# The last head pair's scan is moved into the output stage's program, with part of the output stage's first heads spread over its chunks

## The reference, cut to what matters

```python
def step(state, inp):                      # over the chunks of a sequence, per head
    qd, qkc, uc, wc, kd, gl = inp
    v_new = uc - einsum('bhcd,bhde->bhce', wc, state)
    o = einsum('bhcd,bhde->bhce', qd, state) + einsum('bhcs,bhse->bhce', qkc, v_new)
    state = state * gl[..., None, None] + einsum('bhcd,bhce->bhde', kd, v_new)
    return state, o
...
o = rms_norm(o, norm_w) * silu(z)          # per head, over its 128 channels
return o.reshape(bsz, t, nh * dh) @ w_out  # then x = x + gate * y, rms_norm, the second block
```

## Time and profile before

| what | value |
|---|---|
| time, median of three runs | 2098.21 us (2095.83 to 2099.14) |
| time of the profiled execution | 2094.25 us |
| its span, first to last instruction | 2092.4 us |
| PE busy | 1981.1 us, 95% of the span |
| DVE busy | 1291.3 us, 62% |
| ACT busy | 865.7 us, 41% |
| mean granted TensorE clock | 0.983 |

### The profile page before, as it was taken

One profiled execution on the slowest core, in us unless ns is written; L12 is line 12 of the kernel. 1 busy time (PEld: TensorE's weight loads), 2 busy tenths in 40 slices (PEclk: granted clock), 3 DMA queues, 4 the chain that ended last, 5 costly groups with the idle time before them and its releaser, 6 DMA issues.

```text
span 2092.4 us, 29549 instructions
## 1 busy us (share of the span) xinstructions
PE 1981.1 (95%) x11256; PEld 1629.1 (78%) x11256; DVE 1291.3 (62%) x2447; ACT 865.7 (41%) x1392; POOL 136.8 (7%) x114
## 2 busy tenths in 40 slices
PE   5889999999999999969999899999999999999998
PEld 3667878888887878857776788787787888888877
DVE  7776778796869686749625755445455436633543
ACT  5644353544354443149402333535443438600321
POOL 0020202021111212000000000000000000000000
PEclk8999999999999999989999999999999999999999
DMA  7222323232323242548213131211313115211232
GB/s 286 83 76 70 96 80 107 66 101 71 105 68 102 71 121 67 170 146 289 89 43 139 44 103 32 89 72 61 101 32 111 70 73 210 90 51 42 88 112 81
DMA packets 130252, 204.47 MB, mean 98 GB/s; under 512 B 56853, under 2 KB 88341, under 8 KB 129089
## 3 DMA queue, kind: packets, MB, share of 16 engines
q1 hardware_dynamic: 130112, 202.58, 30.6%
HBM read 156.22 MB, written 42.11 MB: 95 GB/s over the span
## 4 chain that ended last, share of the span: by engine, by line
PE 43%; DVE 6%; ACT 3%; issue 2%; DMA 1%; SPq 0%; DVEq 0%; ACTq 0%
PE m_job L1708 5%; PE m_job L1710 5%; PE m_job L1709 5%; PE e_b L2421 4%; PE e_b L2422 4%; PE e_b L2423 4%; PE p_out L1352 2%; PE p_out L1353 2%; PE p_out L1354 2%; PE p_s L1991 1%; PE e_b L2492 1%; PE e_b L2491 1%; PE e_b L2490 1%; PE p_t L1980 1%; PE p_sc L1968 1%
## 5 line engine op out<-in xcount | busy, mean ns | idle before, releaser
L795 PE MATMUL p_job<-h_hi,w_hi 128*128 128x512 f32 x768 | 321.9, 419 | 16.7 <-DVE h_lo L185 15.2
L797 PE MATMUL p_job<-h_hi,w_lo 128*128 128x512 f32 x768 | 302.9, 394 | 0.0
L796 PE MATMUL p_job<-h_lo,w_hi 128*128 128x512 f32 x768 | 302.5, 394 | 0.0
L1708 PE MATMUL m_job<-h_hi,m_hi 128*128 128x512 f32 x576 | 244.4, 424 | 5.0 <-issue 4.2
L1710 PE MATMUL m_job<-h_hi,m_lo 128*128 128x512 f32 x576 | 227.3, 395 | 0.0
L1709 PE MATMUL m_job<-h_lo,m_hi 128*128 128x512 f32 x576 | 226.1, 392 | 0.0
L795 PEld LDWEIGHTS p_job<-h_hi,w_hi 128*128 128x128 f32 x768 | 146.1, 190 | 58.3 <-issue 16.2
L796 PEld LDWEIGHTS p_job<-h_lo,w_hi 128*128 128x128 f32 x768 | 146.2, 190 | 35.1 <-issue 7.6
L797 PEld LDWEIGHTS p_job<-h_hi,w_lo 128*128 128x128 f32 x768 | 146.0, 190 | 31.3
L633 ACT ACTIVATE pre<-p_job 128x512 f32<-128x512 f32 x96 | 56.8, 592 | 177.5 <-PE p_job L797 174.3
L1708 PEld LDWEIGHTS m_job<-h_hi,m_hi 128*128 128x128 f32 x576 | 109.1, 189 | 25.1 <-issue 5.4
(11 more groups left out here) (399 smaller groups left out, 4224.4 us busy)
## 6 DMA issues: line engine op xcount, KB each, us to landing
w_raw<-in_w SPq DMA_DIRECT2D x49, 512.0 KB
m_raw<-in_w SPq DMA_DIRECT2D x49, 512.0 KB, 3.6
rows<-grows SPq DMA_DIRECT2D x32, 512.0 KB, 6.7
ada<-in_ada_w SPq DMA_DIRECT2D x8, 1024.0 KB, 5.6
z_scr<-pre SPq DMA_DIRECT2D x16, 512.0 KB, 2.6
o_scr<-oT SPq DMA_DIRECT2D x64, 128.0 KB, 1.8
ob<-o_scr SPq DMA_DIRECT2D x16, 512.0 KB, 4.7
zb<-z_scr SPq DMA_DIRECT2D x16, 512.0 KB, 4.9
```

What stands on the lines that cost most here:

```text
L795: nc.tensor.matmul(bank, hi, h_hi[:, k, cut], start=(k == 0), stop=False)
L796: nc.tensor.matmul(bank, hi, h_lo[:, k, cut], start=False, stop=False)
L797: last = nc.tensor.matmul(bank, lo, h_hi[:, k, cut], start=False, stop=(k == KD - 1))
L1708: nc.tensor.matmul(bank, hi, h_hi[:, k, cut], start=(k == 0), stop=False)
```

## The change

The last pair's scan leaves `plan(8)` (the steps stand there only while a next pair exists) and becomes a function `stage_last_scan`, called inside the output stage's streams. Its order on each engine is that of a chunk before; after chunk c, at a named place, a hook of the output stage runs. The first program no longer waits for the stored z and o at its end; SP waits for them where they are needed. Heads 0 to 2 get buffers of their own for squares, heads 0 and 1 for inverse norms and sums (`p_out[4:6]`), and the first two weight splits go to `m_hi`, `m_lo`.

```diff
+def stage_last_scan(nc, io, keep, t):
...
+            for a in range(2):                                   # ACT, chunk c
...
+                nc.scalar.activation(vn[:, a, :], p_head[a][:, P:2 * P], ACT.Copy).then_inc(vn_done, 1)
+            hook(c, 0)
...
+            nc.scalar.activation(oT[:, c % 2], p_query, ACT.Copy).then_inc(o_done, 1)
+            hook(c, 1)
...
+            last.then_inc(write_ready, 1)                        # PE, end of chunk c
+            hook(c)
...
+            for a in range(2):                                   # DVE, chunk c
...
+                                               vb[:, c, a, :], ALU.mult, ALU.add).then_inc(d_done, 1)
+            hook(c)
...
+                nc.vector.scalar_tensor_tensor(S[:, a, :], S[:, a, :], gl[:, c, a:a + 1], p_head[a][:, 2 * P:3 * P],
+                                               ALU.mult, ALU.add).then_inc(s_done, 1)
```

```diff
+            def ahead(c, place):          # ACT; squares are Square and a rounding Copy
+                if (c, place) == (1, 0):   square(0)
+                elif (c, place) == (1, 1): high_square(0)
+                elif (c, place) == (2, 0): square(1)
+                elif (c, place) == (2, 1): high_square(1)
+                elif (c, place) == (3, 0): logarithm(0)
+                elif (c, place) == (3, 1): exponent(0)
+                elif (c, place) == (4, 0): root()
+                elif (c, place) == (5, 0): logarithm(1)
+                elif (c, place) == (5, 1): exponent(1)
+                elif (c, place) == (6, 0): high(0)
+                elif (c, place) == (6, 1): square(2)
+                elif (c, place) == (7, 0): high_square(2)
...
+            def ahead(c):                 # PE
+                if c == 2:
+                    pe.wait_ge(fn_set, 2)
+                    sums(0)
+                elif c == 4:
+                    sums(1)
...
+            def ahead(c):                 # DVE
+                if c == 1:   constants()
+                elif c == 2: low_square(0)
+                elif c == 3: gated(0)
+                elif c == 4: low_square(1)
+                elif c == 5: scaled(0)
+                elif c == 6: gated(1)
+                elif c == 7: low_part(0)
```

```diff
+            scan["scalar"](act, ahead)
+            high(1)
+            for n in range(2, V_HEADS):
+                logarithm(n)
+                exponent(n)
+                if n + 1 < V_HEADS:
+                    square(n + 1)
+                    high_square(n + 1)
+                high(n)
...
+            scan["vector"](dve, ahead)
+            split(0)
+            scaled(1)
+            split(1)
+            low_square(2)
+            low_part(1)
+            gated(2)
             for m, (q, n) in enumerate(steps):
...
+                if q == 0 and n >= 2:
+                    scaled(n)
+                if m >= 2:
+                    split(m)
+                if q == 0 and n >= 2:
+                    if n + 1 < V_HEADS:
+                        low_square(n + 1)
+                    low_part(n)
                     if n + 1 < V_HEADS:
                         gated(n + 1)
```

More of the change, by code:

```diff
@@ L318, in plan @@
         send(2)
-        if q == 3:
+        if q == 3 and ahead:
             out.append(("read", 0))
         send(2)
-    for c in range(NT):
+    for c in range(NT if ahead else 0):
         b, odd = c // 2, c % 2
@@ L1140, with stage_out @@
 CH_PASS = (3, 3, 2)
-def stage_out(nc, io, keep, own):
+def stage_out(nc, io, keep, own, scan):
     if True:
@@ L1256, in square @@
                     act.wait_ge(ss_done, n - 1)
[L1257 to L1265, removed]
@@ L1266, in scalar, with high_square @@
-            nc.scalar.activation(both[:], both[:], ACT.Exp, scale=0.5).then_inc(both_set, 1)
-            for n in range(V_HEADS):
+                if n == EARLY:
+                    act.wait_ge(scan["written"], NT)
+                    act.wait_ge(scan["state"], 2 * NT)
+                    for q in range(2):
+                        act.wait_ge(keep["o_stored"][q], 16 * QK_HEADS * NT // 2)
+                nc.scalar.activation(o_square(n), ob[:, n % 3, :], ACT.Square).then_inc(sq_done, 1)
+            def high_square(n):
+                act.wait_ge(sq_done, 2 * n + 1)
+                nc.scalar.activation(o_parts(n)[0], o_square(n), ACT.Copy).then_inc(sq_done, 1)
@@ L1268, in scalar, with logarithm @@
+            def logarithm(n):
                 act.wait_ge(ss_done, n + 1)
-                if n >= 1:
+                if n >= 3:
                     act.wait_ge(y_done, n)
+                if n == 2:
+                    act.wait_ge(scan["state"], 2 * NT)
+                    for q in range(2):
+                        act.wait_ge(keep["o_stored"][q], 16 * QK_HEADS * NT // 2)
                 for i in range(2):
-                    nc.scalar.activation(rinv[:, i * HALF:(i + 1) * HALF], p_ss[i][:], ACT.Ln,
+                    nc.scalar.activation(inverse(n)[:, i * HALF:(i + 1) * HALF], o_sum(n)[i][:], ACT.Ln,
@@ L1345, in tensor @@
                         sums(n + 2)
-                    hi, lo = w_hi[:, m % 2, c * P:(c + 1) * P], w_lo[:, m % 2, c * P:(c + 1) * P]
+                    if m == 0 and c == 1:
+                        pe.wait_ge(scan["out"], NT)
+                    hi, lo = (part[:, c * P:(c + 1) * P] for part in w_parts(m))
                     for i in range(2):
@@ L1426, in vector @@
[L1426 to L1434, removed]
-            for m, (q, n) in enumerate(steps):
[L1436 to L1446, removed]
+                hi, lo = o_parts(n)
@@ new lines, in ahead @@
+            def ahead(c):
+                if c == 1:
+                    constants()
+                elif c == 2:
+                    low_square(0)
+                elif c == 3:
+                    gated(0)
+                elif c == 4:
+                    low_square(1)
+                elif c == 5:
+                    scaled(0)
+                elif c == 6:
+                    gated(1)
+                elif c == 7:
+                    low_part(0)
+            scan["vector"](dve, ahead)
@@ L1791, in scalar @@
             act.wait_ge(lam, 2)
-            nc.scalar.activation(ld[:], ld[:], ACT.Exp).then_inc(lam_a, 1)
+            nc.scalar.activation(ld[:], ld[:], ACT.Exp).then_inc(lam, 1)
             for i in range(N_IT):
@@ L2637, in stage_after @@
         with first:
-            out = stage_out(nc, io, keep, first)
+            out = stage_out(nc, io, keep, first, scan)
         with second:
```

243 lines of the change are left out of this document (193 added, 50 removed).

## The result

The changed kernel takes 2100.85 us (median of 14 runs, 2099.03 to 2103.9), the kernel before in the same comparison 2096.66 (14 runs, 2091.78 to 2100.52). The ratio is 1.0021, 95% interval [1.0013, 1.0029]: 4.4 us slower, between 2.7 and 6.1. The profiled execution took 2101.58 us, span 2099.7, mean granted clock 0.988.

A forecast was written before the change was run, and what follows sets the result against it. Pass 0, limited by DVE before, would be bound by the ring: 101.9 us from E against 103.7, -1.8; with E's delay of 5.5 that is +3.7 on the median 2098.21, so 2102 us, range 2095 to 2110.

The forecast's parts named there:

- ring: Pass 0: sums, Ln, Exp, scaling, split, low square wait on each other in a loop; 6.97 us a head instead of 5.59.
- E: The end of the scan's last state update, 915.31 us in the kernel before; forecast near 920.8 after the change.
- E to head 2's low square: Start of the output stage on DVE: two splits, a scaling and a low square before the loop, 4.0 us.
- hop, sums to scaling, scaling to low part: End of pass 0, behind the 13 rounds: hop and start 0.16, then 3.59 and 3.58, together 7.3 us.
- barrier and chunk 0, as chunk 1's read: Scan start: with the barrier before the scan, chunk 1's read comes at 896.78 instead of 893.37, +3.4 us.
- sums of heads 0 and 1: In the scan, before a chunk's read on PE: four matmuls, 0.9 us, twice, +1.8 us.
- `Ln` and constants: In the scan: two Ln on ACT too long for their slot, +0.2 us; constants landing late for chunk 1, +0.1 us.
- Rival 1: Pass 0: the ring does not bind, heads keep DVE's 5.59 us; -14 us, 2084; chance 0.17.
- rival 2: Pass 0: PE's clock falls in the ring's gaps, sums take double; 2108 to 2115 us; chance 0.15.
- E's delay: Later end of the moved scan: 3.4 + 1.8 + 0.2 + 0.1 = 5.5 us.
- The slots: Idle times in the scan, ACT 1.08 and 1.20, DVE 1.40 us, said to hold the placed operations except sums and Ln.
- Rival 3: Scan: slots do not hold the work (3.5 us) or the program starts cold (up to 1.6 more); 2107; chance 0.11.

The follow-up runs named there:

- experiment 1: Changed kernel with pass 0's squares two heads ahead again from head 4 on: 2082.98 us, ratio 0.9929 to the kernel before.
- experiment 2: Kernel before with pass 0's squares one head ahead instead of two: 2115.83 us, ratio 1.0078 to the kernel before.
- experiment 4: Changed kernel with seven already-passed semaphore waits a chunk put back into the last scan: 2101.68 us, one run.
- experiment 3: Changed kernel with PE, ACT and DVE work of heads 0 to 2 done behind the scan, not in its slots: 2114.49 us, ratio 1.0076 to kernel before.
- experiment 6: Changed kernel with four unused matmuls at the end of PE's first program, ahead of the barrier: 2099.03 us, one run.
- experiment 5: Changed kernel with DVE's split(n) put behind low_square(n + 1) instead of ahead of it: 2099.89 us, one run.
- experiment 7: Changed kernel with squares two heads ahead, four unused matmuls before the barrier, constants loaded before the first two o loads: 2083.62 us, ratio 0.9939 to kernel before.

## Why the prediction was right

The forecast was 2102 us, 3.8 over the median of before that it started from; measured were 2100.85 and a difference of 4.4 [2.7, 6.1]. (That a difference under 4.2 us can't be told from none was too careful: with 14 runs of each kernel the interval reaches 1.7 us to either side.) Its mechanism, a gain at the stage's start that a ring of queues takes back head by head, is what the runs show: experiment 1 opens the ring in the changed kernel and experiment 2 closes it in the kernel before.

| term | predicted | measured in the trace |
|---|---|---|
| E to head 2's low square | 4.0 | 4.0 (924.16 + 1.22 - 921.37) |
| ring, 13 rounds | 90.6 (6.97 each) | 90.7 (6.977) |
| hop, sums to scaling, scaling to low part | 7.3 | 7.3 (the rest of 102.04) |
| barrier and chunk 0, as chunk 1's read | +3.4 | +4.3 (898.80 - 1.15 - 893.37) |
| sums of heads 0 and 1 | +1.8 | +2.0 |
| `Ln` and constants | +0.3 | +0.8 (nearly all of it the constants) |
| chunks 1 to 7, shorter without the passed waits | 0 | -2.2 |
| sum: net against before | +3.7 | +3.3 |

- **The ring.** The period was put together from five pieces of one passage in which the pipeline was only filling, plus the hop to PE and the longer first matmul (the pieces as stated add up to 6.96, not 6.97). It held to 0.02 us in each of 13 rounds, which took 6.97 to 6.99. Summed: 102.04 us from E against 101.9. Rival 1 (2084) is out: scalings 5.6 apart needed the two-head distance of experiment 1. One of the signs named for it did not come: `low_square` does not wait in the changed kernel, DVE's one wait of a round stands before the scaling.
- **The clock in pass 0.** It is 1.00 through every window of it, with PE idle 1.64 us once per head; rival 2 is out. The Trainium skill's section "HAM oscillation — how this bites in real kernels" ("TensorE: Matmul & The Clock Gate") describes a loop whose waits for DMA are longer than its bursts of matmuls. This loop is not that case: it waits 1.64 of 6.98 us, and no round falls. At the start of the scan the fall is seen after a single idle stretch of 2.45 us (0.79 and 0.72), which is shorter than the gaps that section warns of. Of the two gaps that the prediction read, the second stretch of the earlier trace rows ends at 1437.0, before its gap does (1437.25), and so does not show what came after; the trace does, 1.00 from 1437 to 1442 us, and behind the 2.73 us gap 0.74 from 1142.15 to 1145.
- **E's delay: right sum, wrong parts.** The sentence that put chunk 1's read at 3.10 behind chunk 0's took the chunk at full clock; at 0.79 and 0.72 it took 4.17, 1.1 more. Against that, the barrier was 0.2 cheaper (PE's first read 893.48 with the shift of 1.15 taken out, 893.68 predicted). The constants landed 6.7 us after the program's first issue (894.65 to 901.39), not 5.4, and make chunk 1 some 0.7 longer (3.53 against 2.8) where 0.1 was forecast. And "a gain is excluded, since nothing placed into a slot shortens the chain around it" was wrong: the moved scan carries fewer waits than the steps of before, and chunks 1 to 7 are about 0.3 us shorter each, some 2.8 instead of 3.10 where nothing else lengthens them. (The -2.2 of the table, like +2.0 and +0.8, is reckoned from that 2.8: 3.81 and 3.79 for the chunks with sums, 3.53 for chunk 1, 2.86 for chunk 6.) The two `Ln`, forecast at 0.2, cost nothing that shows: chunks 3 and 5, where they stand, take 2.78 and 2.77. Experiment 4 gives 0.2 to 0.3 a chunk back. (In experiment 3, with nothing placed into them, chunks 2 to 6 take 2.86 us each, as chunk 6 does here; by that base the missing waits are worth 1.7 us and the added terms less, with the same sum.) The errors, +0.9, +0.2, +0.5 and -2.2, cancel to -0.6 (4.91 measured, 5.5 predicted); that the total came so close is luck. Of the two terms at the start the constants are the one that counts: with the clock at 1.00 in experiment 6 DVE only waits longer for them, 3.04 us against 1.56, and chunk 2's read comes no earlier.
- **The slots.** Sums cost 1.0 each, at the two places named; ACT's and DVE's operations fit. Experiment 3 puts all placed work together at 2.5 us. Rival 3 is out, though its "cold start" exists, with 1.3 us in chunk 0 (4.17 against 2.83 in experiment 6), in the clock and not in the barrier, which took 1.47 us from SP's last issue to PE's first read (893.16 to 894.63) against the 1.57 of before; behind it the constants would have made the scan wait all the same.

What stays open: why the constants take 6.7 us to land (6.4 to 6.9 in experiments 1, 4, 5 and 6, which load them in the same order); experiment 7 moved them ahead but did not separate the queue from the loads beside it. Which of the seven waits of experiment 4 costs how much was not tried.

## What to carry to other kernels

When work of a stage is moved ahead to fill a gap, keep the distance in heads between a value and its use, and follow one value once around through every in-order queue: if the walk comes back to its own start, and no engine has more work than that in a round, its length is the period, however idle the engines look. A gain that comes once (19.5 us at the start: E to head 2's scaling 27.25 before, 7.76 after) is used up by 1.38 us a round in 14 rounds; here 13 were left, and E's own delay of 4.9 us decided the sign. A saving ahead of a later wait, as in experiments 6 and 7, is worth only what that wait does not swallow.

## What was not expected of the hardware

- Waits on events that have long come are not free on a chain of short operations: seven of them took 0.2 to 0.3 us of a 2.8 us chunk (experiment 4), seen in the idle time as 0.49 instead of 0.32 us ahead of `Dl` and 0.44 instead of 0.19 ahead of solve.
- An idle stretch of PE of 2.45 us at the barrier was followed by a first chunk at clocks of 0.79 and 0.72 (4.17 us); one of 1.54 us at the same place by 1.00 (2.83 us); in experiment 3 one of 3.92 us by matmuls of 0.63 instead of 0.39. All five kernels here with 2.44 or 2.45 us of idle time at the barrier took 4.13 to 4.53 us for chunk 0, both with 1.54 us (experiments 6 and 7) 2.83. Idle stretches of 1.64 us once per head left pass 0 at 1.00.
